# Sliding-window attention in a two-layer hybrid decoder: scores of 64 queries by 192 keys, mask inside the contraction

## The reference, cut to what matters

```python
kb, vb = band(k), band(v)          # previous block of 128 and own block: 256 keys
scores = einsum('bnqhgd,bnkhd->bnhgqk', qb, kb) * (HEAD_DIM ** -0.5)
delta = qi + WINDOW - kj           # query position - key position
valid = (delta >= 0) & (delta < WINDOW) & (blk * WINDOW + kj - WINDOW >= 0)
scores = where(valid, scores, -inf)
m = maximum(max(scores), sink)
p = exp(scores - m)
probs = p / (sum(p) + exp(sink - m))
out = einsum('bnhgqk,bnkhd->bnqhgd', probs, vb)
```

## Time and profile before

| | |
|---|---|
| median of 3 runs | 2533.83 us (2532.74 to 2868.94) |
| profiled execution | 2530.34 us |
| its span, slowest core (core 4) | 2529.3 us (all cores: 2520.4 to 2529.3) |
| mean granted TensorE clock | 0.990 on that core, 0.990 to 0.994 on all |
| PE busy | 2464.3 us (97%), 12322 matmuls |
| DVE busy | 1427.2 us (56%) |
| ACT busy | 1185.1 us (47%) |
| POOL busy | 450.2 us (18%) |
| DMA | 221.97 MB moved, mean 88 GB/s |

### The profile page before, as it was taken

One profiled execution on the slowest core, in us unless ns is written; L12 is line 12 of the kernel. 1 busy time (PEld: TensorE's weight loads), 2 busy tenths in 40 slices (PEclk: granted clock), 3 DMA queues, 4 the chain that ended last, 5 costly groups with the idle time before them and its releaser, 6 DMA issues.

```text
span 2529.3 us, 35812 instructions; the slowest of 8 cores (2520.4 to 2529.3 us)
## 1 busy us (share of the span) xinstructions
PE 2464.3 (97%) x12322; PEld 1127.8 (45%) x12322; DVE 1427.2 (56%) x2244; ACT 1185.1 (47%) x1970; POOL 450.2 (18%) x488
## 2 busy tenths in 40 slices
PE   5999999999999999999999999999999899999998
PEld 1444444444444444444444444444444344444443
DVE  4167443799647543599927544379955664433112
ACT  2165984411126797422106699541114669823111
POOL 0041234000004223200003223400000322330000
PEclk8999999999999999999999999999999999999999
DMA  7122247533552336734364225743336323373433
GB/s 158 34 51 51 51 101 164 99 71 73 114 121 51 54 60 130 160 74 81 61 150 85 50 51 108 169 91 74 67 69 134 71 51 63 70 156 67 79 58 90
DMA packets 48769, 221.97 MB, mean 88 GB/s; under 512 B 4688, under 2 KB 4944, under 8 KB 37840
## 3 DMA queue, kind: packets, MB, share of 16 engines
q0 software_dynamic: 26496, 163.59, 36.7%
q1 hardware_dynamic: 22096, 56.10, 6.9%
HBM read 366.47 MB, written 16.78 MB: 152 GB/s over the span
## 4 chain that ended last, share of the span: by engine, by line
PE 92%; DMA 3%; ACT 2%; DVE 2%; issue 1%; POOL 0%; SPq 0%; DVEq 0%; ACTq 0%; POOLq 0%
PE psum L782 91%; DMA arena<-x 2%; PE psum L786 1%; DVE arena L850 1%; DMA y<-arena 1%; ACT arena L816 1%; ACT L816 1%; DMA arena<-rope 1%; DVE arena L843 0%; DVE arena L833 0%; ACT arena L822 0%; POOL arena L833 0%; SPq L868 0%; DVEq L156 0%; DVE arena L1050 0%
## 5 line engine op out<-in xcount | busy, mean ns | idle before, releaser
L782 PE MATMUL psum<-arena 128*128 128x512 bf16 (+4 forms) x11826 | 2441.5, 364 | 51.2 <-ACT arena L816 23.5
L782 PEld LDWEIGHTS psum<-arena 128*128 128x128 bf16 (+2 forms) x11826 | 1099.0, 98 | 1373.6 <-issue 129.9
L833 DVE TENSOR_TENSOR arena<-psum,arena 128x512 f32<-128x512 f32 (+1 forms) x576 | 387.5, 687 | 553.8 <-PE psum L782 306.2
L850 DVE SCALAR_TENSOR_TENSOR arena<-arena 128x1024 f32<-128x1024 bf16 (+3 forms) x648 | 615.7, 991 | 53.5 <-ACT arena L816 44.9
L816 ACT ACTIVATE arena<-psum 128x512 bf16<-128x512 f32 (+1 forms) x536 | 311.3, 597 | 655.3 <-PE psum L782 653.2
L816 ACT ACT_TABLE_LOAD x318 | 408.0, 1283 | 64.2 <-PE psum L782 44.2
L833 POOL TENSOR_TENSOR arena<-arena 128x512 bf16<-128x512 f32 (+1 forms) x264 | 329.8, 1256 | 439.6 <-DVE arena L833 403.6
L816 ACT ACTIVATE arena<-arena 128x512 bf16<-128x512 f32 (+3 forms) x356 | 194.7, 576 | 278.9 <-DVE arena L833 236.8
L833 DVE TENSOR_TENSOR arena<-arena,psum 128x512 f32<-128x512 f32 (+1 forms) x160 | 109.0, 686 | 275.3 <-PE psum L782 273.5
L822 ACT COPY arena<-psum 128x1024 bf16<-128x1024 bf16 (+2 forms) x96 | 81.5, 849 | 180.0 <-PE psum L782 122.6
L816 ACT ACTIVATE arena<-psum,arena 128x256 bf16<-128x256 f32 (+3 forms) x284 | 138.4, 489 | 57.4 <-PE psum L782 54.0
(11 more groups left out here) (17 smaller groups left out, 161.4 us busy)
## 6 DMA issues: line engine op xcount, KB each, us to landing
arena<-wgu POOLq DMA_DIRECT2D x44, 1024.0 KB, 8.8
arena<-win POOLq DMA_DIRECT2D x48, 768.0 KB, 7.5
arena<-win POOLq DMA_DIRECT2D x28, 1024.0 KB, 10.5
arena<-wdn POOLq DMA_DIRECT2D x32, 704.0 KB, 6.6
arena<-x SPq DMA_DIRECT2D x24, 512.0 KB, 9.5
arena<-wbr POOLq DMA_DIRECT2D x16, 768.0 KB, 9.8
arena<-wout POOLq DMA_DIRECT2D x8, 1024.0 KB, 13.5
xmid<-arena SPq DMA_DIRECT2D x16, 512.0 KB, 8.9
```

The lines of the kernel that those rows point to most:

```text
L782: return ((lambda: nc.tensor.matmul(o.ap, lhsT=l.ap, rhs=r.ap, start=start, stop=stop)), [l, r], [o])
L833: vec(eng, o, nel(a), lambda: eo.tensor_tensor(out=o.ap, in0=a.ap, in1=b.ap, op=op), [a, b], shift=shift)
L850: vec("dve", o, nel(a), lambda: nc.vector.scalar_tensor_tensor(out=o.ap, in0=a.ap, scalar=(sc.ap if isinstance(sc, Ref) else sc), in1=b.ap ...
```

## The change

The unit stays one block of 128 queries by one key head, but is now cut into two sub-blocks e of 64 queries, each with the 192 keys that it can see. Two query heads stand side by side in the 128 columns of the stationary operand. The contraction has 128 rows: 64 of the head's features, and 64 that hold a one-hot code of the query's place (`hot`, in `qa`) against the mask's rows (`band`, in `ka`); so the mask is added without matmuls of its own. These constants come by four DMAs in each half (`fills`, 64 partitions each, on POOL's queue), and q and k are copied by DVE from a temporary into the other 64 rows (two copies in `q_unit`, `put_k` for k, which writes each run of 64 keys three times). `qa` lies over `yglu` and `cacc` (the convolution's buffers), `ka` over the xn buffer that the half does not use, which in half 0 holds two of the `diag` tiles.

`att_b` still has 8 transposes, of which four are now of 64 columns; `att_c` has two groups of four matmuls of V, alternately over 128 and over 64 keys, each group with a bank and an ACT copy of its own. The heads' order in `yAt` changes, and with it the host's layout of the branch weights and of the sinks. The arena grows from 206000 to 212832 bytes a partition, `kT` (2304 bytes) goes. The planner's bookkeeping no longer takes a landed DMA as proof that the instructions before it on its queue are done.

```diff
-            c2[("eng", eng)] = max(c2.get(("eng", eng), 0), op.seq - 1)
...
-SBN = 206000
+SBN = 212832
...
-    qT = fixed([4, HT], BF16, XS0)
+    qa = [fixed([2, 16, 2, 64], BF16, XS0 + r * 8192) for r in range(2)]
+    KA = [[fixed([3648], BF16, XN[i].off + r * 7296) for r in range(2)] for i in range(2)]
...
-            cp("pool", kT[:, 0:128], kT[:, HT:HT + 128])
+            put_k(khist[:, 0:128], 0, 2)
             cp("pool", V[:, 0, :], V[:, 8, :])
+        ka = KA[(H + 1) % 2]
+        def fills():
+            for r in range(2):
+                rows = slice(64 - r * 64, 128 - r * 64)
+                for t, d, n in ((qa[r], hot_d, 4096), (ka[r], band_d, 3648)):
...
+                    dma("pool", to, d[rows], [], [t[rows]], "fill%d%d" % (r, n), 64 * n * 4)
+        def put_k(src, b0, nb):
+            for r in range(2):
+                rows = slice(r * 64, r * 64 + 64)
+                o = ka[r][rows, b0 * 192:(b0 + nb) * 192].re(lambda a: a.rearrange("p (b r t) -> p b r t", r=3, t=64))
+                i = Ref(src.tile, rows, src.fk, lambda a: a.rearrange("p (b r t) -> p b r t", r=1, t=64).to_broadcast([64, nb, 3, 64]))
+                vec("dve", o, nb * 192, lambda o=o, i=i: nc.vector.tensor_copy(out=o.ap, in_=i.ap), [i], 2.0)
...
         def q_unit(j, b):
-            rope(w3(W["q"], 0, 8, 512), j, b, qT[:, j, b * NB:(b + 1) * NB])
+            qt = bft()
+            rope(w3(W["q"], 0, 8, 512), j, b, qt.all())
+            for k in range(2):
+                rows = slice(k * 64, k * 64 + 64)
+                cp("dve", qa[k][rows, j // 2, b * 8:(b + 1) * 8, j % 2, :], qt[rows].re(lambda a: a.rearrange("p (b t) -> p b t", t=64)))
         def k_unit(b):
-            rope(w3(W["kv"], 0, 8, 256), 0, b, kT[:, 128 + b * NB:128 + (b + 1) * NB])
+            kt = bft()
+            rope(w3(W["kv"], 0, 8, 256), 0, b, kt.all())
+            put_k(kt[:, 0:512], 2 + b * 8, 8)
+            if b == 1:
+                cp("dve", khist.all(), kt[:, 384:512])
...
         def att_a(t):
-            for g in range(4):
-                parts.append(mmp(sc[:, g * nk:(g + 1) * nk], qT[pr, g, n * 128:(n + 1) * 128], kT[pr, k0:k0 + nk], True, False))
-                parts.append(mmp(sc[:, g * nk:(g + 1) * nk], identb.all(), amb[:, 256 - nk:256], False, True))
-            pe(parts, [nk] * 8, reserve=2)
+            nks = (64, 128) if lone else (192, 192)
+            for e in range(2):
+                i, nk = n * 2 + e, nks[e]
+                nr = nk // 64
+                sc = bank((2, nk))
+                kv = ka[hh][:, k0:k0 + nr * 256].re(lambda a, nr=nr: a.rearrange("p (r c) -> p r c", r=nr)[:, :, 0:64])
+                pe([mmp(sc[:, p, :], qa[hh][:, p, i, :, :].re(lambda a: a.rearrange("p g t -> p (g t)")), kv, True, True) for p in range(2)],
+                   [nk] * 2, reserve=1)
+                vec("dve", A(2 * e, 2 * e + 2), 2 * nk, lambda e=e, sc=sc: nc.vector.tensor_reduce(
+                    out=A(2 * e, 2 * e + 2).ap, in_=sc.all().ap, axis=AX.X, op=ALU.max), [sc.all()])
...
         def att_b(t):
+            p = bank((6, 128), BF16)
             for pr in range(2):
+                if not lone:
+                    parts.append(trp(p[:, pr, :], pu[:, pr, 0:128]))
+                    parts.append(trp(p[64:128, 4 + pr, :], pu[:, 2 + pr, 0:64]))
+                parts.append(trp(p[:, 2 + pr, :], pu[:, 2 + pr, 0:128] if lone else pu[:, 2 + pr, 64:192]))
+                parts.append(trp(p[0:64, 4 + pr, :], pu[:, pr, 0:64] if lone else pu[:, pr, 128:192]))
...
         def att_c(t):
+            for e in range(2):
+                o = bank((2, 64))
+                for pr in range(2):
+                    rows = slice(pr * 64, pr * 64 + 64)
+                    if lone:
+                        todo = [[(V[lo, 1, hs], pt[lo, 4 + pr, :])], [(V[:, 1, hs], pt[:, 2 + pr, :])]][e]
+                    elif e == 0:
+                        todo = [(V[:, n, hs], pt[:, pr, :]), (V[lo, n + 1, hs], pt[lo, 4 + pr, :])]
+                    else:
+                        todo = [(V[:, n + 1, hs], pt[:, 2 + pr, :]), (V[hi, n, hs], pt[hi, 4 + pr, :])]
+                    for i, (v, x) in enumerate(todo):
+                        parts.append(mmp(o[rows, :, :].re(lambda a: a.rearrange("p g t -> p (g t)")), v, x, i == 0, i + 1 == len(todo)))
+                pe(parts, [128] * len(parts), reserve=0)
+                acopy(yAt[:, hh * 2:hh * 2 + 2, n * 128 + e * 64:n * 128 + e * 64 + 64], o.all())
...
-        unit(T["qkv"] - 0.5, hist)
+        unit(q0 - 0.7, fills)
+        unit(q0 - 0.6, hist)
```

More of the change, by code:

```diff
@@ L646, in _host_layout @@
     consts[:, C_M01:C_M01 + 128] = (s_i <= t_i).astype(f)
[L647 to L652, removed]
-    consts[:, C_NF:C_NF + 8] = inp["norm_final"].reshape(8, 128).T
+    consts[:, C_NF:C_NF + 8] = inp["norm_final"].reshape(8, 128).T
+    r_i = np.arange(128) % 64
+    c_i = np.arange(64)
+    hot = np.tile((r_i[:, None] == c_i[None, :]).astype(f), (1, 64))
+    band = np.zeros((128, 19, 3, 64), f)
+    band[:, :, 0, :] = np.where(c_i[None, :] <= r_i[:, None], -30000.0, 0.0)[:, None, :]
+    band[:, :, 2, :] = np.where(c_i[None, :] > r_i[:, None], -30000.0, 0.0)[:, None, :]
     m_i = np.arange(128)
@@ L743, in build_program @@
     mergedT = fixed([8, HT], BF16, R1 + 24576)
-    PU = [fixed([4, 256], BF16, mergedT.off + r * 2048) for r in range(4)]
-    PT = [fixed([1024], BF16, mergedT.off + 8192 + r * 2048) for r in range(4)]
+    PU = [fixed([4, 192], BF16, mergedT.off + r * 1536) for r in range(5)]
+    PT = [fixed([6, 128], BF16, mergedT.off + 7680 + r * 1536) for r in range(5)]
     diag = [fixed([31, 128], BF16, (R1 + 24576, XN[1].off)[i // 2] + i % 2 * 7936) for i in range(4)]
-    kT = fixed([128 + HT], BF16)
     V = fixed([9, 128], BF16)
@@ L986, in hist @@
                 return
-            cp("pool", kT[:, 0:128], kT[:, HT:HT + 128])
+            put_k(khist[:, 0:128], 0, 2)
             cp("pool", V[:, 0, :], V[:, 8, :])
+        ka = KA[(H + 1) % 2]
[3 more added lines that the diff above has]
+                for t, d, n in ((qa[r], hot_d, 4096), (ka[r], band_d, 3648)):
+                    to = t[rows]
+                    if len(t.shape) > 1:
+                        to = to.re(lambda a: a.rearrange("p a b g t -> p (a b g t)"))
+                    dma("pool", to, d[rows], [], [t[rows]], "fill%d%d" % (r, n), 64 * n * 4)
[5 more added lines that the diff above has]
+                vec("dve", o, nb * 192, lambda o=o, i=i: nc.vector.tensor_copy(out=o.ap, in_=i.ap), [i], 2.0)
         def ropes():
@@ L1029, in att_a @@
             lone = first and n == 0
[L1030 to L1035, removed]
-            for g in range(4):
-                parts.append(mmp(sc[:, g * nk:(g + 1) * nk], qT[pr, g, n * 128:(n + 1) * 128], kT[pr, k0:k0 + nk], True, False))
-                parts.append(mmp(sc[:, g * nk:(g + 1) * nk], identb.all(), amb[:, 256 - nk:256], False, True))
-            pe(parts, [nk] * 8, reserve=2)
-            s3 = sc[:, 0:4 * nk].re(lambda a: a.rearrange("p (g k) -> p g k", g=4))
-            A = lambda lo, hi: ast[:, t % 6, lo:hi]
-            vec("dve", A(0, 4), 4 * nk, lambda: nc.vector.tensor_reduce(out=A(0, 4).ap, in_=s3.ap, axis=AX.X, op=ALU.max), [s3])
+            nks = (64, 128) if lone else (192, 192)
+            A = lambda lo, hi: ast[:, t % 6, lo:hi]
+            scs = []
+            for e in range(2):
+                i, nk = n * 2 + e, nks[e]
+                nr = nk // 64
+                sc = bank((2, nk))
+                scs.append(sc)
+                k0 = i * 192 + (3 - nr) * 256
+                kv = ka[hh][:, k0:k0 + nr * 256].re(lambda a, nr=nr: a.rearrange("p (r c) -> p r c", r=nr)[:, :, 0:64])
[3 more added lines that the diff above has]
+                    out=A(2 * e, 2 * e + 2).ap, in_=sc.all().ap, axis=AX.X, op=ALU.max), [sc.all()])
             stt(A(4, 8), A(0, 4), -0.125, nsinks[l][:, hh * 4:hh * 4 + 4], ALU.mult, ALU.min)
             tt(A(12, 16), A(4, 8), sm[:, SM_SINK + hh * 4:SM_SINK + hh * 4 + 4], ALU.add)
-            pu = PU[t % 4]
-            for g in range(4):
-                act(pu[:, g, 0:nk], sc[:, g * nk:(g + 1) * nk], AF.Exp, bias=A(4 + g, 5 + g), scale=0.125, accum=A(8 + g, 9 + g))
+            pu = PU[t % 5]
+            for e in range(2):
+                for p in range(2):
+                    g = e * 2 + p
+                    act(pu[:, g, 0:nks[e]], scs[e][:, p, :], AF.Exp, bias=A(4 + g, 5 + g), scale=0.125, accum=A(8 + g, 9 + g))
             act(A(16, 20), A(12, 16), AF.Exp)
@@ L1051, in att_a @@
             for g in range(4):
-                ts(pu[:, g, 0:nk], pu[:, g, 0:nk], A(24 + g, 25 + g), ALU.mult, rate=4.0)
-            att[t] = (n, hh, lone, nkb, nk)
+                ts(pu[:, g, 0:nks[g // 2]], pu[:, g, 0:nks[g // 2]], A(24 + g, 25 + g), ALU.mult, rate=4.0)
+            att[t] = (n, hh, lone)
         def att_b(t):
[L1056 to L1066, removed]
+            n, hh, lone = att[t]
```

(32 more changed lines are left out.)

19 lines of the change are left out of this document (11 added, 8 removed).

## The result

The changed kernel takes 2570.51 us (median of 4 runs, 2569.78 to 2795.8) against 2533.28 us: 1.0148 times the time before, 95% interval 1.0125 to 1.0171. Some launches of most versions run some per cent longer, with a lower granted clock on the cores of one die; the ratios and intervals of this document leave them out. Slower was forecast, 2550 us; the measured time is inside the range, but the loss is 37 us where 17 were forecast.

What follows compares the result with a forecast made beforehand. PE's issue time was taken as the bound. Full units +20 us and lone units -3 made +17, the other terms 0: 2530.3 + 17 = 2547, with the median 3.5 above, written as 2550 us; range 2506 to 2574.

Steps and rivals of the forecast that it cites:

- The bound: Whole kernel: PE's own issue time is the kernel's time, one for one; PE busy 97% of the span.
- Part 1, att_a: Score matmuls of a unit: 8 of 256 columns become 4 of 192 without shape switches, gain 1.38 us a unit.
- Part 2, att_b: Transposes of a unit: alternately 128 and 64 columns, each followed by a shape switch, loss 0.78 us a unit.
- Part 3, att_c: V matmuls of a unit: 8 alternating over 128 and 64 rows, 1.39 us against 0.45, loss 0.94 us.
- the lone units: Four units beside the 60 full ones: fewer score-stage switches, some new ones later, -0.65 us each, -3 us in all.
- rival A: V matmuls: height may change for nothing within the 64-column shape, 45 us less, 2505 us; chance 0.13.
- D: Rival on the transposes: those of 64 columns run as full ones, no switch cost, 47 us less, 2503 us; chance 0.05.
- Part 6, the DVE copies: q and k copies on DVE: together 42 us, hidden except short waits at q units, +1 us a half, +4.
- Parts 4 and 5, the fills: Constant DMAs of each half: 13 to 16 us inside 24 us in half 0, hidden in halves 1 to 3; cost nothing.
- Rival B: Fills not hidden, PE waits: 2570 us for half 0 alone, 2597 at worst; chance 0.12.
- Part 7: ACT work a little shorter and fp32 temporary slots from 6 to 10: fewer short waits, -4 us; dropped bookkeeping line 0.
- Rival C: Switches as forecast, but new order and extra slots remove 10 to 20 us of waits: 2535 us; chance 0.10.

## Why the prediction was wrong

- **The bound** held. PE's issue time is the kernel's time: the table's +41.9 us of PE stand against +40.3 of span, and the switches taken out of the changed kernel came back nearly one for one (58 us of 60, 53 of 55 to 58, 45 of 47). In the q/k/v stages it did not hold: there PE waits for DVE.
- **Part 1, att_a**, held: 0.33 us, gain 1.38.
- **Part 2, att_b, was mis-sized**: loss 0.88 us a unit (1.34 less 0.45), forecast 0.78. **Part 3, att_c, too**: 1.46 us, forecast 1.39, so the loss is 1.01 where 0.94 stood. Together 0.17 to 0.2 us x 60, so 10 to 12 of the missing 20 us; the lone units, forecast at -3, gave 0 to -1. The count of switches was right (9 in part 3, where 1.39 us stood for 9.5). The price was not: 98 to 100 ns instead of 110 (transposes: 1.34 - 0.45 = 0.89 over 8) and 113 (V: 1.46 - 0.45 = 1.01 over 9). The step that failed is the reading of the earlier trace rows. I took the entry as 93 and the exit as 0.16 less 0.06, and laid all the rest of the part on streaming. But the 8 matmuls of `att_c` ran in pairs: four pairs stream 4 x 56 = 0.22 us, and the whole part took 0.45, so its two switches cost 0.22 us, 110 ns each. Part of this sits inside, not at the edge: from 361.69 to 361.88 three pairs take 0.19 us where 0.17 would stream (by single starts 80, 56 and 56 ns). A price has to come from the whole stretch less what streams in it. The runs show this price in its place: 8 transposes in two groups instead of in turn save 0.79 us, 0.66 us for 6 switches and 0.11 for two pairs that run together again. The inner switch of height at 64 columns, which no row had shown, costs as much as the others: its lower bound (nothing) and with it rival A are ruled out, and D is too, by transposes 168 ns apart.
- **Part 6, the DVE copies, was the other miss**: called hidden, +4 us. Their sum was 54 us instead of 42: the q copies took 43.9 instead of 22, those of k 10.5 instead of 19. The step that failed here is the price of a q copy: 0.35 us between two rows, with nothing for POOL's work beside it, where 0.69 was measured; with it the overlap failed. Of the 32 q units 26 have a copy that is held by a POOL sum; there the two copies take 1.35 to 1.65 us, with 1.29 us of products 2.6 to 2.9 us against PE's 1.94. The forecast had 2.07. The row of waits is 11 us longer; with the copies on ACT 16 us of it go. The rates of a stage must be compared unit by unit: DVE was at 60 of 80 us in the window and still the slower engine while the q units ran.
- **Parts 4 and 5, the fills**, held: nothing waits for them but 0.9 us of DVE. Rival B is wrong in its cause. Its 2570 us for half 0 alone is the measured time by luck: the 20 us came from the price of the switches and from DVE's copies.
- **Part 7**: the slots give 7 us, forecast 4 with ACT's part. Rival C is wrong: the slots and the new order did not shorten the waits on balance, they grew.

The balance in PE's time: 17 forecast, 31 measured for streaming, switches and pairs (-33.7 + 53.4 + 11.3), and 0 forecast, 11 measured for waits. So the mechanism was right, a slower kernel by switches of shape, and two sizes were off by about as much each: 10 to 12 us by the price of a switch, 11 by the waits. The median moved by 37 of these 42. What is left open is the late wait at the last half's entry: it was 8.9 us before, 11.4 in the changed kernel and 13.0 with the copies on ACT, and between the cores of one execution it differs more, its longest piece from 2.5 to 9.2 us before the change.

## What to carry to other kernels

Order matmuls by the shape of their tile: on this kernel each change of height or width costs about 110 ns, as much as 256 columns, so that eight matmuls in turn took two and a half to three times what the same eight took in groups (1.34 against 0.55 us, 1.46 against 0.51). When a change removes work from the bound engine, count the switches that its new order brings as carefully as the columns that it saves; here the columns gave 34 us, and the switches with the pairs that no longer ran together took 65. And compare engines at the unit that repeats, with DVE copies priced beside POOL's work, not alone.

## What the runs showed of the hardware

- A change of shape costs 105 to 113 ns of PE whatever changes (128 rows to 64, 128 columns to 64, or 64 rows within 64 columns), at full granted clock. A change of both at once, the exit of the grouped V matmuls, was priced only together with two others: 0.34 us for the three. Within one shape, matmuls on different tiles run together: four 64 x 64 ones start 3 to 4 ns apart, two on column halves 7 before the change and 3 in the grouped orders.
- A score matmul over 64 rows streams as fast as one over 128: 109 ns for 256 columns once it follows its like.
- A DVE copy of 64 x 512 bf16 takes 0.27 to 0.29 us, and 1.04 to 1.36 when it starts while a POOL sum of 1.26 us runs (mean of all 64: 0.69). One that repeats its input three times takes 0.55 us for 1536 elements written and 0.25 for 384, means of the trace in which POOL has no sum beside them: 0.26 ns an element and a fixed part, where the maximum over scores takes 1.05, in spite of the 64-element runs.
- ACT loaded its tables 318 times before and 176 times after, 182 us less of ACT. PE's waits for ACT's functions stayed at 23.5 and 24.5 us; no run isolates what the loads did to the time.
